# Moving the 32 memory half jobs of each layer of a fused decoder trunk: 12 into the differential attention steps, 6 into sparse units 1 and 2, 14 into later sparse units

## The reference

```
proj = rms_norm(h) @ w_in                # split into q_a k_a v_a q_i k_i w_i q_b k_b v_b, rotary on q and k
out_a = per query: the 256 keys with the best index score, softmax(q_a k_a) v_a    # 8 heads of 64, one shared key/value head
out_b = (softmax(q1 k1) - lam * softmax(q2 k2)) v_b                                # 4 heads, differential, causal
h = h + concat(out_a, norm(out_b)) @ w_out
k, v = split(rms_norm(mem) @ w_kv)       # mem: 256 tokens; w_kv 1024 x 2048
h = h + softmax(q k) v @ w_o             # 4 memory heads of 256
h = h + (silu(conv(g)) * u) @ w_down     # ConvGLU, width 2816
```

## Time and profile before

| | us |
|---|---|
| median of 3 runs | 3224.66 |
| lowest and highest | 3222.22, 3224.84 |
| the profiled execution | 3224.33 |
| its span, first to last instruction | 3222.5 |
| PE busy in the span | 3054.0 (95%) |
| differential stages, layer 0 and 1 (from the trace) | 296 to 427, 1873 to 2005 |
| sparse stages | 427 to 621, 2005 to 2199.5 |

### The profile page before, as it was taken

The page is one execution under the profiler, slowest core; times in us unless marked ns, Lnnn a source line. Parts: engine busy times, 40 slices in busy tenths (PEclk is TensorE's granted clock), DMA queues, the critical chain, the costliest instruction groups (busy, mean ns, idle before and its releaser), DMA issues.

```text
span 3222.5 us, 40481 instructions
## 1 busy us (share of the span) xinstructions
PE 3054.0 (95%) x15272; PEld 2541.6 (79%) x15272; DVE 2079.0 (65%) x3457; ACT 1452.0 (45%) x2430; POOL 751.7 (23%) x386
## 2 busy tenths in 40 slices
PE   7998889899999999999999987899999999999998
PEld 5787877788887888878877977777887788887887
DVE  6677876442459999942448688663443799998234
ACT  6368955532344333321324788554332533333112
POOL 1122035322021222232221300542211122222221
PEclk8998999999999999999999989999999999999999
DMA  6554812321022222252254474224111122324322
GB/s 207 163 151 109 180 40 58 117 62 46 15 58 65 92 79 79 80 169 77 92 138 127 120 165 110 58 59 127 40 33 46 46 79 81 97 79 133 96 74 77
DMA packets 313794, 300.00 MB, mean 93 GB/s; under 512 B 19824, under 2 KB 275312, under 8 KB 313344
## 3 DMA queue, kind: packets, MB, share of 16 engines
q1 hardware_dynamic: 305312, 280.63, 30.4%
q10 hardware_dynamic: 8288, 16.78, 1.6%
HBM read 219.71 MB, written 77.66 MB: 92 GB/s over the span
## 4 chain that ended last, share of the span: by engine, by line
PE 74%; DVE 11%; ACT 9%; issue 3%; DMA 2%; POOL 1%; SPq 1%; DVEq 0%; ACTq 0%; POOLq 0%
PE ps L2126 37%; PE ps L2397 8%; PE ps L2399 8%; PE ps L2398 8%; ACT above L1035 4%; PE ps L2161 3%; PE ps L2318 2%; PE ps L2256 1%; PE ps L2310 1%; ACT p_a L1190 1%; PE ps L2193 1%; PE ps L2194 1%; PE ps L2371 1%; DVE xs_lo L1437 1%; DVE p_a L1824 1%
## 5 line engine op out<-in xcount | busy, mean ns | idle before, releaser
L887 POOL TENSOR_TENSOR w_lo<-raw,w_hi 128x1024 fp32r<-128x1024 f32 (+4 forms) x172 | 362.3, 2111 | 1133.0 <-ACT w_hi L957 1131.4
L2126 PE MATMUL ps<-xs_hi,w_hi 128*128 128x512 f32 (+1 forms) x1728 | 540.7, 394 | 19.7 <-POOL w_lo L887 14.0
L2126 PE MATMUL ps<-xs_lo,w_hi 128*128 128x512 f32 (+1 forms) x1728 | 536.0, 392 | 0.0
L2126 PE MATMUL ps<-xs_hi,w_lo 128*128 128x512 f32 (+1 forms) x1728 | 535.0, 391 | 0.0
L1863 DVE TENSOR_TENSOR h_t<-h_t,ps 128x1024 f32<-128x1024 f32 x96 | 117.2, 1221 | 495.3 <-PE ps L2126 487.7
L2126 PEld LDWEIGHTS ps<-xs_hi,w_hi 128*128 128x128 f32 (+1 forms) x1728 | 323.4, 189 | 97.3 <-issue 20.6
L2126 PEld LDWEIGHTS ps<-xs_lo,w_hi 128*128 128x128 f32 (+1 forms) x1728 | 325.8, 189 | 71.2
L2126 PEld LDWEIGHTS ps<-xs_hi,w_lo 128*128 128x128 f32 (+1 forms) x1728 | 324.7, 188 | 70.6
L957 ACT ACTIVATE w_hi<-raw 128x1024 fp32r<-128x1024 f32 (+4 forms) x148 | 124.7, 851 | 468.0 <-PE ps L2126 412.3
L915 POOL TENSOR_SCALAR p_a<-p_a,rca 128x1024 f32<-128x1024 f32 (+7 forms) x96 | 181.8, 1903 | 469.0 <-DVE rca L1797 468.4
L2397 PE MATMUL ps<-xs_hi,w_hi 128*128 128x512 f32 x672 | 262.0, 390 | 3.2 <-DVE xs_lo L1959 3.2
(11 more groups left out here) (343 smaller groups left out, 6260.5 us busy)
## 6 DMA issues: line engine op xcount, KB each, us to landing
raw<-in_w_gu SPq DMA_DIRECT2D x48, 512.0 KB, 4.5
act_spill<-cv SPq DMA_DIRECT2D x44, 512.0 KB, 6.0
raw<-in_w_in SPq DMA_DIRECT2D x32, 512.0 KB, 5.5
qk_spill<-t_hi SPq DMA_DIRECT2D x24, 512.0 KB, 2.6
qk_spill<-t_lo SPq DMA_DIRECT2D x24, 512.0 KB, 2.8
k_b<-qk_spill SPq DMA_DIRECT2D x32, 384.0 KB
gate_e<-in_w_gu SPq DMA_DIRECT2D x20, 512.0 KB, 4.1
up_e<-in_w_gu SPq DMA_DIRECT2D x20, 512.0 KB, 5.4
```

The source lines that it names most:

```text
L887: nc.gpsimd.tensor_tensor(w_lo[s][:, w], raw[s][:, w], w_hi[s][:, w].bitcast(f32), ALU.subtract).then_inc(lo_done, 1)
L2126: ins = M(dst[0:c, a:b], w[s][:, k * c:(k + 1) * c], xt[:, a:b], start=(at == 0 and w is w_hi and part == 0), stop=(at == kc - 1 and w is ...
```

## The change

The table of half jobs is written anew. 12 jobs stand in differential steps: one each in steps 12 to 19 (short blocks, around the turn from head 1 to head 2) and 28 to 31. Sparse units 1 and 2 keep three each. Units 3 to 7, 9, 11 and 13 have none. Units 8, 10, 12 and 14 (first groups, no VA) have two each as before, unit 15 gets two, and four stand at v = 16, behind the last unit's scores and ahead of its transposes. On SP, `memory_done` of slices 0 and 1 stands between the loads of head 2 and head 3, that of slices 2 and 3 behind head 3, and the first two loads of the sparse queries (`load_sparse(0, 4)`, `load_sparse(4, 7)`) behind them. The line `prev = None` keeps DVE from doing the last unit's reciprocal twice.

```diff
-KV_B = {}
-KV_A = {1: [0, 1, 2], 2: [3, 4, 5], 3: [6, 7, 8], 4: [9, 10, 11], 5: [12, 13], 6: [14, 15], 7: [16, 17], 8: [18, 19], 9: [20, 21], 10: [22, 23], 11: [24, 25], 12: [26, 27], 13: [28, 29], 14: [30, 31]}
+KV_B = {12: [0], 13: [1], 14: [2], 15: [3], 16: [4], 17: [5], 18: [6], 19: [7], 28: [8], 29: [9], 30: [10], 31: [11]}
+KV_A = {1: [12, 13, 14], 2: [15, 16, 17], 8: [18, 19], 10: [20, 21], 12: [22, 23], 14: [24, 25], 15: [26, 27], 16: [28, 29, 30, 31]}
...
                 load_later_head(2)
+                for f in range(0, 2):
+                    memory_done(f)
+                load_later_head(3)
+                for f in range(2, 4):
+                    memory_done(f)
                 load_sparse(0, 4, qa_dma)
-                load_later_head(3)
                 load_sparse(4, 7, qa_dma)
                 after(sp, thr_done, 1)
...
                 load_sparse(7, 8, qa_last)
-                for f in range(0, 2 * KC):
+                for f in range(4, 2 * KC):
                     memory_done(f)
...
                         normalise(*prev)
                         scale_probabilities(*prev)
+                        prev = None
```

## The result

The changed kernel takes 3206.46 us (median, 3204.47 to 3208.39). The kernel before took 3224.44 us (3222.22 to 3224.84) beside it. The ratio is 0.9946 with a 95% interval of 0.9928 to 0.9963: 17 us or 0.5% faster, where 3203 was predicted.

The account below looks back on a forecast made before the run. PE, busy 95%, was taken as the bound. Layer 0: 24.8 - 12.6 - 1.2 - 1.9 = 9.1 us; layer 1: 9.1 + 2.75 = 11.9; together 21 of 3224.3, giving 3203 us, range 3187 to 3217.

Parts of the forecast that it names:

- The bound: PE is busy for 95% of the span; half jobs take 1.79 us each, nearly all on the path.
- What leaves the sparse units: 18 jobs leave units 3 to 7, 9, 11 and 13: 24.8 us gained in layer 0, 1.9 lost to one clock fall.
- rival 2: Exponential chain replaces the half jobs in even units; units 4 and 6 give nothing: 3217 us, chance 0.07.
- Rival 3: All eight thinned sparse units fall to a lower clock, 27 us back: 3229 us, no change; chance 0.08.
- What the differential steps pay: 12 half jobs in steps 12 to 19 and 28 to 31 cost 12.6 us in layer 0, between 6 and 21.5.
- the coupling of the tiles: Steps 13 to 15: next step's second score waits for DVE to drain the half job's tile; 0.8 us taken.
- Rival 4: Differential steps: scores, V, T and ACT wait behind half jobs, 3.0 us each; includes late loads; 3250 us, chance 0.08.
- Rival 1: Differential jobs are hidden too, all 12 costing 6 us: 3190 us, chance 0.07.
- Steps 17 to 20 without waits: Sign expected in the changed profile: PE has no waits there, and step-20 scores come 9 us later.
- a DMA as releaser of the half job: Sign that would show the prediction wrong: PE's half job line (L2161) released by a DMA.
- The end: Six jobs in units 15 and 16 cost 1.2 us; VA of the last pair in about 1 us, not 2.72.
- Layer 1's wait for head 3: PE's 2.75 us wait for head 3's queries goes: less load lies ahead, first use moves back 9 us.

Follow-up runs that it names:

- experiment 4: Three runs with the half jobs of steps 16 to 19 moved to units 4 and 6: on the base 3212.24 us; on e7, 3197.29 (e9) and 3188.11 (e12).
- experiment 5: Four runs on the half jobs' place inside sparse units: e7 3177.59 us, e11 3182.25, e10 3224.92, and units 1 and 2 of the base respread, 3191.62.
- Experiment 2, e3: Changed kernel with each differential step's half job behind that step's V and T, not ahead: 3192.97 us, ratio 0.9897 to the kernel before.
- experiment 3: Jobs of units 15 and 16 (six), or 16 (four), put back earlier in the changed kernel: 3204.74, 3210.31 us; the six in the base: 3197.89.
- experiment 1: Kernel before with head 3's loads issued ahead of the sparse queries of heads 0 to 3: 3226.24 us, ratio 0.9999.
- e7: The base with a sparse unit's half jobs behind its first three score tiles, not ahead of them: 3177.59 us, ratio 0.985 to the kernel before.
- e12: e7 with the half jobs of steps 16 to 19 in units 4 and 6, sparse queries held until step 24's second score: 3188.11 us.
- e11: e7 with unit 1's third half job behind the first pair of transposes: 3182.25 us, ratio 0.9865 to the kernel before.
- the base: Changed kernel with each differential step's half job behind that step's V and T: 3192.97 us, ratio 0.9897 to the kernel before.
- e10: Kernel before, its 32 half jobs kept in their units but placed behind each unit's first three score tiles: 3224.92 us, ratio 0.9997.
- e9: e7 with the half jobs of steps 16 to 19 in units 4 and 6, sparse queries held until step 20's last score: 3197.29 us.

## Why the prediction was right, and where it was off

- **The bound.** Right. A half job taken out of units 3 to 7 gave 1.5 to 1.7 us of its 1.8, and PE stayed at 95%.
- **What leaves the sparse units, 24.8 less 1.9 for the clock.** Right in sum: 23.4 and 22.6 against 22.9. From the half jobs of unit 2 to VA of unit 3, unit 3 gave 4.9 and 5.2 (5.0 predicted). By the starts of VA, units 4 and 5 together 7.6 (7.2), units 6 and 7 6.2 (5.6). Units 8 to 13 gave 5.2 and 3.6 where 5.1 were left to them. Ahead of unit 2's jobs layer 0 lost 0.6. So the even units were not held by the exponential chain, and rival 2 falls; in experiment 4 four jobs put back there cost 5.2 to 6.6 us, not nothing.
- **Rival 3, the clock.** It did not hold for all eight units, and the one fall of 1.9 us was too few: VA of units 11 and 13 in layer 0 ran slow (5.35 for 16 products, 4.49 for 12), 1.7 us each, VA of units 9 and 13 in layer 1 (1.5 and 1.7). Against this stands the fall at unit 9 of layer 0, which went. I had priced a fall from that one row; in layer 1 of the same trace the two jobs took 3.84 us behind the same wait of 1.84. The Trainium skill's rule on bursts that alternate with waits ("TensorE: Matmul & The Clock Gate", "HAM oscillation — how this bites in real kernels") bore on the late odd units, and not on units 3 to 7. The traces agree in part. Ahead of VA in units 9, 11 and 13 stood one wait of 1.8 us each in both layers, in units 4 to 7 none over 0.8; in experiment 5, where the longest is 0.9, the same work ran at 1.00. But of the six VA behind a wait of 1.8 us four were slow and two were not.
- **What the differential steps pay, 12.6.** Right in sum within 1.3 us (13.7, and 13.9 with the wait of layer 1 taken out of before), and in part by luck, since errors of both signs met in it. By the starts of V, step 12 cost 1.7 in both layers (1.8 predicted), steps 13 to 15 3.2 (0.8), step 16 1.0 and 1.1 (2.1), steps 17 to 19 5.0 and 3.5 (4.3). Experiment 2 shows that the place ahead of V was to blame in steps 12 to 15, where the same jobs behind V and T cost nothing. Steps 13 to 15 were sized at 0.8 for the coupling of the tiles; that is the mis-sized term. The coupling came in as I described it, score behind the copy, V and T behind the score, ACT behind them, but as waits of 1.84 and 1.96 us and a half job at the lower rate. Steps 12 to 20 together cost 10.9 and 9.4, not 9.0. Rival 4 was right as a mechanism, and at 13.8 us for 12 jobs, 1.15 each, far from its price of 3.0 and from the 1.92 at which it decides.
- **Rival 1.** Twelve jobs at 6 us were not seen, but 7.6 to 8.0 were, once the jobs stood behind V and T (experiment 2). That most of the cost lay in the order within the step is what I had not asked.
- **Steps 17 to 20 without waits** was wrong: in layer 0 a half job waited 1.43 us for its weights, issued at 376.27, just ahead of the loads of head 3. I had named a DMA as releaser of the half job as a sign of error; it was a small one, in one layer.
- **The end, 1.2.** It cost 1.5 and 2.3. VA of the last pair came down from 2.72 to 1.83, not to 1. The exchange of units 9, 11 and 13 for 15 and 16 was worth 2 us a layer by four traces, about half of what my terms said (experiment 3), and the times don't tell it from zero.
- **Layer 1's wait for head 3, 2.75.** Gone, by the trace of the change and of experiment 1. My reason (less ahead of it, and a later first use) is half of it. Experiment 4 shows the other half: half jobs 4 to 7 stand in SyncE's list between head 3 and the sparse queries and hold these back, and that use is 5 us later because of those jobs (e7 and e12 from V of step 11 to V of step 23: 46.9 and 41.4 us). Without both it waits 7 us. I had filed that delay under rival 4, as a risk. The hold is only in part a wait for the jobs. In e7's timeline of SyncE one write of `kv_st` takes 8.69 us to issue (7.76 in the changed kernel, layer 0) while the loads of head 3 are under way, and the write before it 0.37:

```profile
376.07 0.43 SPq L689 DMA_DIRECT2D v_pair<-v_spill  x1
376.60 0.37 SPq L705 DMA_DIRECT2D kv_spill<-kv_st  x1
...
381.11 8.69 SPq L705 DMA_DIRECT2D kv_spill<-kv_st  x1
...
390.74 8.97 SPq L646 DMA_DIRECT2D q_a<-qk_spill  x12
```

What stays open: why the clock fell at one unit in one layer and at another in the next, and in one execution but not in another with the same work (experiment 1). There is one trace of each kernel, and such a fall moved the start of a step by 2.1 us, so single differences of that size between traces prove little. Open too is what makes head 3 late in e12, and the third half job of unit 1 in experiment 5, which still waits 2.58 us, since e11 moved it without a gain.

## What to carry to other kernels

Filling a stage's idle time with foreign work has two choices, which step and where inside the step, and here the second was worth more: the same jobs cost 13.8 us or 7.8 in the same steps, depending on whether they stood ahead of or behind what ACT waits for, and behind the scores of sparse units 1 and 2 the chain they had delayed hid part of them. Before placing such work, write down which buffer of the ring each following operation will now inherit, and when its reader lets go. And a wait in a DMA queue that seems only to delay loads may be protecting an earlier one: look at what is issued next when it goes.

## What the runs showed of the hardware

- The same work ran at different clocks, by its place among the waits: 379 matmuls of the late sparse units took 60.05 us at a granted clock of 0.95 with a wait of 1.8 us ahead of each VA of units 9, 11 and 13 (the base), and 56.62 us at 1.00 with none over 0.9 us (e7); 12 products of values took 4.49 us or 2.79.
- It differed between executions too: with the same jobs in these steps, the granted clock from 1945 to 1955 us was 0.97 in the kernel before and 0.53 in e10.
- And it differed from layer to layer of one execution: in the base VA of unit 9 took 5.77 us in layer 0 and 4.51 in layer 1.
- To issue a DMA is not always short: twelve loads of the sparse queries took 15.59 us to issue in e9 and 4.53 in e12, one write of `kv_st` 8.69 us in e7 and 0.37 just before.
- The same edit was worth 15 us in one placement (e7 against e3) and nothing in another (e10 against before).
